# A square root of one constant column, run on ScalarE ahead of each norm's squares, in a two-block transformer kernel

## The reference, cut to what matters

```
def rms_norm(x, g):
    xf = x.astype(jnp.float32)
    y = xf * lax.rsqrt(jnp.mean(xf * xf, axis=-1, keepdims=True) + EPS)
    return (y * g.astype(jnp.float32)).astype(x.dtype)
```

## Time and profile before

| | us |
|---|---|
| median of 3 runs | 2171.61 (2166.54 to 2173.66) |
| profiled execution, its own time | 2173.97 |
| its span, first to last instruction | 2172.2 |
| PE busy | 1958.8 (90%) |
| DVE busy | 678.0 (31%) |
| ACT busy | 534.1 (25%) |
| mean granted TensorE clock | 0.942 of full |

### The profile page before, as it was taken

One profiled execution on the slowest core, in us unless ns is written; L12 is line 12 of the kernel. 1 busy time (PEld: TensorE's weight loads), 2 busy tenths in 40 slices (PEclk: granted clock), 3 DMA queues, 4 the chain that ended last, 5 costly groups with the idle time before them and its releaser, 6 DMA issues.

```text
span 2172.2 us, 30456 instructions
## 1 busy us (share of the span) xinstructions
PE 1958.8 (90%) x11646; PEld 1321.2 (61%) x11646; DVE 678.0 (31%) x1489; ACT 534.1 (25%) x967; POOL 47.7 (2%) x64
## 2 busy tenths in 40 slices
PE   5877999999999999987789999999999999999976
PEld 2744679987979987974654444444444444444436
DVE  3554166504436712434421111111111110111124
ACT  3235155303335502434311111111111110111123
POOL 0100001100001100000000000000000000000000
PEclk8988999999999999978869999999999999999988
DMA  8344555345454434400349999999999999999960
GB/s 341 133 176 195 213 195 193 138 153 203 165 195 174 177 137 155 168 18 1 119 189 418 422 422 421 422 422 422 421 422 422 422 422 422 422 422 422 422 282 20
DMA packets 83781, 592.43 MB, mean 273 GB/s; under 512 B 9120, under 2 KB 11680, under 8 KB 12032
## 3 DMA queue, kind: packets, MB, share of 16 engines
q1 hardware_dynamic: 83424, 589.77, 67.5%
q10 hardware_dynamic: 288, 1.71, 0.2%
HBM read 590.39 MB, written 1.05 MB: 272 GB/s over the span
## 4 chain that ended last, share of the span: by engine, by line
DMA 25%; PE 24%; ACT 1%; DVE 1%; issue 1%; SPq 1%; ACTq 0%; DVEq 0%
DMA ring<-in_experts 24%; PE ps L1897 15%; PE ps L1885 2%; PE ps L1908 1%; PE ps L1511 1%; PE ps L1512 1%; PE ps L1515 1%; PE ps L1568 1%; PE ps L1923 1%; SPq L525 0%; DMA ring<-in_weights 0%; DVE rstd L965 0%; PE ps L1875 0%; DVE aT L980 0%; PE ps L1842 0%
## 5 line engine op out<-in xcount | busy, mean ns | idle before, releaser
L1897 PE MATMUL ps<-ring,A 128*64 128x512 f32 x3168 | 700.6, 595 | 51.6 <-ACT A L878 31.7
L1897 PEld LDWEIGHTS ps<-ring,A 128*64 128x64 f32 x3168 | 247.9, 137 | 480.5 <-issue 480.5
L1511 PE MATMUL ps<-aL_hi,wd_hi 128*128 128x256 f32 x1152 | 305.8, 300 | 22.5 <-DVE aL_lo L992 14.3
L1512 PE MATMUL ps<-aL_lo,wd_hi 128*128 128x256 f32 x1152 | 296.4, 292 | 0.0
L1410 DVE TENSOR_TENSOR A<-ps,W 128x512 f32<-128x512 f32 x66 | 45.4, 688 | 793.5 <-PE ps L1923 793.5
L1511 PEld LDWEIGHTS ps<-aL_hi,wd_hi 128*128 128x128 f32 x1152 | 230.3, 200 | 34.1 <-issue 16.3
L959 DVE TENSOR_TENSOR wd_lo<-ring,wd_hi 128x2048 fp32r<-128x2048 f32 x81 | 185.5, 2297 | 150.0 <-ACT wd_hi L627 150.0
L1512 PEld LDWEIGHTS ps<-aL_lo,wd_hi 128*128 128x128 f32 x1152 | 231.9, 201 | 0.2
L627 ACT ACTIVATE wd_hi<-ring 128x2048 fp32r<-128x2048 f32 x81 | 153.7, 1905 | 77.8 <-DMA ring<-in_weights 64.3
L1515 PE MATMUL ps<-aL_hi,wd_lo 128*128 128x256 f32 x1152 | 167.0, 289 | 5.7 <-DVE wd_lo L959 5.7
L1695 PE MATMUL ps<-A,ring 128*128 128x256 f32 x704 | 155.9, 385 | 3.8 <-DVE W L1101 3.8
(11 more groups left out here) (269 smaller groups left out, 1673.5 us busy)
## 6 DMA issues: line engine op xcount, KB each, us to landing
ring<-in_experts SPq DMA_DIRECT2D x396, 1024.0 KB, 19.9
ring<-in_weights SPq DMA_DIRECT2D x162, 1024.0 KB, 4.9
tab<-in_tables ACTq DMA_DIRECT2D x1, 1296.0 KB, 8.5
hT<-in_x SPq DMA_DIRECT2D x1, 1024.0 KB, 9.6
hT<-in_ctx SPq DMA_DIRECT2D x1, 1024.0 KB, 11.8
out<-aT SPq DMA_DIRECT2D x1, 1024.0 KB, 3.9
A<-in_tables SPq DMA_DIRECT2D x1, 548.0 KB, 5.8
small<-in_small ACTq DMA_DIRECT2D x1, 377.0 KB, 3.2
```

The source lines that it names most:

```text
L1511: pe.matmul(out, wd_hi[:, b, c, cols], a_hi[:, c, :], start=(c == 0), stop=False)
L1512: pe.matmul(out, wd_hi[:, b, c, cols], a_lo[:, c, :], start=False, stop=False)
L1897: mm = pe.matmul(ps[h * CAP:(h + 1) * CAP, bank, :], x[:, k + c, :], w[:, c, h], start=(first and c == 0), stop=(last and c == 3))
```

## The change

One line is added at the head of ACT's part of each norm. It overwrites a scratch column that nothing reads.

More of the change, by code:

```diff
@@ L642, in norm @@
                 src = hT if src is None else src
+                bring_in(ACT.Sqrt, 0)
                 for c in range(KC):
```

## The result

Nine runs of the changed kernel have a median of 2176.12 us (2174.54 to 2178.54). The ratio is 1.0032, 95% interval 1.0022 to 1.0043. In a second comparison it was 1.0027 (1.0017 to 1.0037), 2176.35 against 2170.69 us. So the change costs 5.7 us by the one comparison and 7.8 by the other (3.7 to 9.3 us by the two intervals). I had forecast +0.9 us (2172.5), and "within 0.3%" as by far the likeliest; the two ratios lie on either side of that line. The time lies in the range; the effect is six times or more what I worked out. The profiled executions hide it: 2173.97 us before and 2175.14 us after, since the one of before took longer than any of its nine.

What follows compares the result with a forecast made beforehand. It took expert-weight DMAs and PE's matmuls to bound the kernel. Terms of -1.56 + 0.99 + 0.99 + 0 gave +0.4 us, or +1.5 with nothing given back; the middle, +0.9, gave 2172.5 us, range 2167 to 2178.5.

Steps and rivals of the forecast that it cites:

- the terms: Per-norm gains and costs, ranging in the forecast from 0 to +3.5 us around 2171.6 us.
- signs of being wrong: Roots 1.3 us behind squares in norms 1, 2, 4; norm 5's first square 2.7 us late; clock below 1.00 where full.
- Old place, 0.52 us: Between last square and root, the load costs 1.31 - 0.79 = 0.52 us; removing it saves that through to the end.
- New place, hidden in norms 1, 2, 4, 3 and 6: Before the first square: 1.5 us hidden in norms 1, 2, 4; only a hidden 0.2 us activation in 3, 6.
- Norm 0: Load fits ACT's 3.43 us wait; squares 0.1 to 0.2 us later, hidden by PE's weights wait: nothing, 0.2 at most.
- Norm 5: the upper bound: ACT itself is late: 1.5 us added, nothing returned if the last sums run at half clock: +1.5 us.
- the middle that I took: Whole-kernel total taken as +0.9 us, between +0.4 and +1.5, as norm 5's sums run partly at either clock.
- Norm 7: Squares follow the second `gate` cell's rounding, all on the chain: +0.99 us, up to +1.5.
- Norm 8: 0.95 of 1.5 us hidden behind the last sigmoid, 0.52 given back at the end: about 0.
- drain behind a load: At table loads, the skill's 1.38 us beside 1.28, 2.66 in all, would make the sum -3.6 us; chance 0.01.
- The slower rival: Longer PE waits at norms 5 and 7 each bring another half-clock stretch: +9.2 us, 2180.8; chance 0.07.
- The faster rival: Shorter gaps in norms 1, 2 and 4 spare low-clock spells, some 4 us each: 2160.5 us; chance 0.03.

Runs made afterwards that it cites:

- f10: Kernel before plus the added activation in norms 1, 2 and 4, with an ACT copy holding norm 4's root back: 2170.78 us, ratio 1.0003.
- e3: Kernel before plus the added activation in norms 1, 2 and 4 alone: 2173.59 us, ratio 1.0007.
- f11: Kernel before plus the added activation in norms 1, 2 and 4 alone, timed again: 2174.42 us against 2169.85, ratio 1.0020.
- e8: Kernel before with loads moved to where ACT waits, for norms 1, 2, 5 and 7 only: 2169.77 us against 2170.69, ratio 0.9994.
- e2: Kernel before plus nine added Copy activations in the same places, no table load moved: 2171.52 us, ratio 0.9998.
- e5: The full change built again, against the kernel before: 2176.35 us against 2170.69.

## Why the prediction was wrong

The number was saved by luck. The range, 2167 to 2178.5 us, was wide enough because it allowed 4 us to either side for the spread of a median; the terms in it ended at +3.5 us, and the change costs 5.7 to 7.8. One of the prediction's own signs of being wrong came: a granted clock below 1.00 where it was full before, 0.72 in the second stretch.

- **Old place, 0.52 us: right.** 0.79 instead of 1.31 us in all of norms 1, 2 and 4.
- **New place, hidden in norms 1, 2, 4, 3 and 6: right.** Norm 0 too: its squares start 0.1 us behind the start of the added activation and PE's later wait for weights swallows it.
- **Norm 5: the upper bound was right, +1.5 us,** not the +0.99 of the sum or the middle that I took. The root does follow the last square after 0.79 us, but the 16 matmuls of the sums take 6.75 us at 0.58 of the clock instead of 6.2 at 0.69, and that eats the 0.52 us. **Norm 7: +1.0, right. Norm 8: -0.06, right.**
- **No drain behind a load.** The next activation starts 0.01 us after it and in the profile after likewise. The 2.66 us of the Trainium skill's section "What ACT_TABLE_LOAD costs" ("ScalarE: Activation LUTs") don't show here.
- **The step that failed is that the terms could be added up at an unchanged clock.** Saving 0.52 us in norm 4 was booked as -0.52. Together with norms 1 and 2 it brings +4 us: the piece behind norm 4 takes 197.8 instead of 193.8 us, with PE at 0.50 instead of 0.88 of its clock in the stretch that begins 168 us behind root 4. The experiments show this by holding the root back alone (f10). Behind root 4 the profiles add up to 4.1, norm 5 at its upper bound 1.5, the piece behind it -0.7 (for which I have no cause), the first expert pass 1.3 and norm 7 1.0, +7.2 us in all. With the -1.56 booked for norms 1, 2 and 4 that makes 5.6, near the 5.7 of the second comparison, but that part is booked and not measured.
- **The slower rival named the clock, but the wrong place.** I looked for it where a wait is added, norms 5 and 7. There it gives 1.3 to 1.8 us. Most of it comes some 168 us behind a place where a wait is taken away. The prediction says that more waiting can only make it worse; f10 waits longer at one place and is faster by 3.6 us. The faster rival holds too, in small: right behind norm 4 the shorter gap does spare low clock, 1.2 us of it, which is gone again 93 us behind root 4.
- **The spread was a sign.** The changed kernel's seventeen runs all lie at 2174.5 us or above, and of 102 runs of the kernel before in the later comparisons 18 do. The runs of the kernel before differ by 11 us and more in each of these comparisons. One reading, which the profiles of e3 and f11 beside f10 support but no run tests for before itself, is that such a kernel has more than one course its clock can take and that a small shift chooses between them.

Two things stay open. Why half a microsecond at norm 4 makes the attention run longer at the lower level was not settled, nor what norms 1 and 2 add to it. I take it to be a matter of when PE's pauses fall against the moments at which the granted clock changes, but that is not shown: no run here varied those moments, and none moved root 4 by several amounts. And the savings of norms 1 and 2 (1.0 us) and of e8 (2 us) are seen at the roots, not in the medians. Even in the profiles they don't always get through: from root 1 to root 4, where norms 2 and 4 should save 1.04 us, e2 takes 576.10 us, e3 and e5 575.03 and 575.00, but the changed kernel and f11 575.93.

## What to carry to other kernels

A table load that runs beside the last matmul of a sum costs only what it sticks out, 0.52 us here and not 1.28. Moving it forward pays where the engine waits anyway and costs the full 1.5 us where the engine itself is late, so the same line doesn't fit every call of a helper. Where PE works in bursts and its clock changes between them, a sum of sub-microsecond terms says little: look at how far the runs of the unchanged kernel lie apart, and take that, not the terms, as the scale of what may come out. And compare stretches counted from the same piece of work, not from the start: the profiles of before and after are 6 us apart at root 4.

## What I had not expected of the hardware

A program that is done earlier in one place can end later. ACT's extra copy of 1.39 us on the path, which delays one root by 0.4 us, saved 3.6 us of 2174 (f10 against f11), because the granted clock was 0.89 instead of 0.50 in 12 us of an attention stage that begin 168 us behind that root (0.50 in f11's profile as in e3's).
